# Normalising the attention probabilities: two scaled identities on GpSimd, or one row multiply each on GpSimd and VectorE

## The reference, cut to what matters

```python
p = jnp.exp(s - m)
denom = jnp.sum(p, axis=-1, keepdims=True) + jnp.exp(sink - m)
o = jnp.einsum('bnkgqs,bnskd->bnqkgd', (p / denom).astype(v.dtype), vb)
```

```python
p_w = masked_softmax(jnp.einsum('bgrqd,bgkd->bgrqk', qb, kw), m_w)
o_w = jnp.einsum('bgrqk,bgkd->bgrqd', p_w.astype(vw.dtype), vw)
return gb[:, 0][..., None] * o_c + gb[:, 1][..., None] * o_s + gb[:, 2][..., None] * o_w
```

## Time and profile before

| what | value |
| --- | --- |
| median of 3 runs | 4002.84 us (4000.92 to 4006.6) |
| profiled execution: span from first to last instruction | 4004.4 us |
| its own time outside the span | not listed; the span stands for it |
| PE busy, share | 3909.7 us, 98% |
| DVE | 2736.3 us, 68% |
| ACT | 1987.8 us, 50% |
| POOL | 212.2 us, 5% |
| mean granted TensorE clock | 0.991 |

### The profile page before, as it was taken

How to read it: one execution, slowest core, us unless ns; L and a number is a source line. 1 busy time by engine, 2 the same in 40 slices (tenths; PEclk the granted TensorE clock), 3 DMA queues, 4 the chain that set the end, 5 groups by cost and what they waited for, 6 DMA issues and landing times.

```text
span 4004.4 us, 78708 instructions
## 1 busy us (share of the span) xinstructions
PE 3909.7 (98%) x34150; PEld 3793.3 (95%) x34150; DVE 2736.3 (68%) x4071; ACT 1987.8 (50%) x2620; POOL 212.2 (5%) x277
## 2 busy tenths in 40 slices
PE   8999999999999999999999999999999999999999
PEld 8979999889998999999997999999998899999999
DVE  6566665666655656567555799956756699974855
ACT  5445444454544545465435545754444544764443
POOL 0011000110002000010023000000000000000000
PEclk9999999999999999999998999999999999999999
DMA  6534555345555455534550455456654455455754
GB/s 237 192 115 151 192 190 190 133 148 195 181 194 182 160 199 184 195 133 173 191 204 34 159 194 181 177 199 233 229 196 153 158 177 193 175 182 202 265 199 158
DMA packets 114791, 720.78 MB, mean 180 GB/s; under 512 B 13328, under 2 KB 13664, under 8 KB 32784
## 3 DMA queue, kind: packets, MB, share of 16 engines
q1 hardware_dynamic: 90144, 652.25, 45.9%
q10 hardware_dynamic: 19200, 37.01, 2.5%
q0 software_dynamic: 5104, 26.49, 1.9%
HBM read 692.48 MB, written 23.22 MB: 179 GB/s over the span
## 4 chain that ended last, share of the span: by engine, by line
PE 87%; DVE 7%; ACT 4%; issue 1%; POOL 0%; DMA 0%; ACTq 0%; DVEq 0%; POOLq 0%
PE psum L655 26%; PE psum L657 26%; PE psum L656 26%; PE psum L1408 3%; DVE slab_low L1916 2%; ACT slab_high L1427 2%; DVE h_parts L2219 1%; PE psum L1065 1%; PE psum L1048 1%; PE psum L875 1%; PE psum L1078 1%; ACT room L1670 1%; DVE room L2248 0%; DVE room L2253 0%; PE psum L1349 0%
## 5 line engine op out<-in xcount | busy, mean ns | idle before, releaser
L1916 DVE TENSOR_TENSOR slab_low<-slab,slab_high 128x2048 fp32r<-128x2048 f32 x622 | 1423.2, 2289 | 738.8 <-ACT slab_high L1427 736.6
L655 PE MATMUL psum<-h_parts,slab_high 128*128 128x256 f32 x5632 | 1578.2, 280 | 28.9 <-DVE h_parts L2219 18.6
L1427 ACT ACTIVATE slab_high<-slab 128x2048 fp32r<-128x2048 f32 x622 | 1189.3, 1912 | 785.4 <-PE psum L657 721.1
L656 PE MATMUL psum<-h_parts,slab_high 128*128 128x256 f32 x5632 | 1556.5, 276 | 0.0
L657 PE MATMUL psum<-h_parts,slab_low 128*128 128x256 f32 x5632 | 1556.1, 276 | 0.0
L655 PEld LDWEIGHTS psum<-h_parts,slab_high 128*128 128x128 f32 x5632 | 1063.5, 189 | 48.8 <-issue 24.0
L655 PE MATMUL psum<-hidden_parts,slab_high 128*128 128x256 f32 x3840 | 1063.5, 277 | 11.4 <-DVE hidden_parts L2166 4.8
L656 PEld LDWEIGHTS psum<-h_parts,slab_high 128*128 128x128 f32 x5632 | 1063.5, 189 | 2.4 <-issue 2.2
L657 PEld LDWEIGHTS psum<-h_parts,slab_low 128*128 128x128 f32 x5632 | 1062.8, 189 | 0.0
L656 PE MATMUL psum<-hidden_parts,slab_high 128*128 128x256 f32 x3840 | 1058.0, 276 | 0.0
L657 PE MATMUL psum<-hidden_parts,slab_low 128*128 128x256 f32 x3840 | 1058.0, 276 | 0.0
(11 more groups left out here) (346 smaller groups left out, 3326.0 us busy)
## 6 DMA issues: line engine op xcount, KB each, us to landing
slab<-in_up SPq DMA_DIRECT2D x176, 1024.0 KB, 4.8
slab<-in_keys_up SPq DMA_DIRECT2D x128, 1024.0 KB, 4.8
slab<-in_keys_down SPq DMA_DIRECT2D x128, 1024.0 KB, 4.8
slab<-in_down SPq DMA_DIRECT2D x88, 1024.0 KB, 4.8
slab<-in_w_in SPq DMA_DIRECT2D x16, 1024.0 KB, 4.8
slab<-in_wq SPq DMA_DIRECT2D x16, 1024.0 KB, 4.8
peer_gates<-room ACTq DMA_DIRECT2D x64, 256.0 KB, 2.3
room<-peer_gates ACTq DMA_DIRECT2D x64, 256.0 KB, 5.4
```

The lines of the kernel that those rows point to most:

```text
L655: nc.tensor.matmul(out, lhs[0], rhs[0], start=first, stop=False, **options)
L656: nc.tensor.matmul(out, lhs[0], rhs[1], start=False, stop=False, **options)
L1427: nc.scalar.activation(k.high[m % PARTS][:, 0:width], k.slabs[m % RING][:, 0:width], ACT.Copy).then_inc(k.rounded.up())
L1916: nc.vector.tensor_tensor(k.low[m % RING][:, 0:width], k.slabs[m % RING][:, 0:width], k.high[m % PARTS][:, 0:width], ALU.subtract).then_in ...
```

## The change

In the first mixers and the sparse stage, the diagonals go. DVE still forms the quotients (reciprocal, and gate product in the sparse stage), now signals them (`quotients`), waits for its own signal, and multiplies the second head's row of probabilities in place. GpSimd waits for the same signal and multiplies the first head's row in place. PE waits for both and turns the rows with `transpose`, as the forgetting stage does. The wait for a stale quotient buffer stays, on the new signal. The buffers of the diagonals go, at the end of their stage's memory, so that nothing else moves. The forgetting stage keeps its instructions; only its DVE step's signal has another name.

```diff
 PE, attend:
-            if "diagonal" in v.items[n]:
-                nc.tensor.wait_ge(k.diagonal_pool.sem, k.diagonal_pool.at(n + 1))
-            else:
-                nc.tensor.wait_ge(k.normed.sem, k.normed.at(n + 1))
+            nc.tensor.wait_ge(k.normed.sem, k.normed.at(n + 1))
+            if "shared" in v.items[n]:
+                nc.tensor.wait_ge(k.normed_pool.sem, k.normed_pool.at(n + 1))
...
-                    if "diagonal" in v.items[n]:
-
-                        mm = nc.tensor.matmul(k.banks[6][:, at:at + P], v.probs[:, n % 5, e, kt * P:(kt + 1) * P], v.diagonals[:, n % 3, e, :],
-                                              start=True, stop=True)
-                        continue
                     mm = nc.tensor.transpose(k.banks[6][:, at:at + P], v.probs[:, n % 5, e, kt * P:(kt + 1) * P], k.const("ident"))
 DVE, normalise:
-            if "diagonal" in it and n >= 6:
-                nc.vector.wait_ge(k.diagonal_pool.sem, k.diagonal_pool.at(n - 5))
-            if "diagonal" in it and "gate" not in it:
-                nc.vector.reciprocal(small[:, 8:10], small[:, 4:6]).then_inc(k.normed.up())
-                continue
-            self.then(nc.vector.reciprocal(small[:, 8:10], small[:, 4:6]))
-            if "diagonal" in it:
-                nc.vector.tensor_tensor(small[:, 8:10], small[:, 8:10], it["gate"], ALU.mult).then_inc(k.normed.up())
-                continue
-            for e in range(2):
+            if "shared" in it and n >= 6:
+                nc.vector.wait_ge(k.normed_pool.sem, k.normed_pool.at(n - 5))
+            quotient = nc.vector.reciprocal(small[:, 8:10], small[:, 4:6])
+            if "gate" in it:
+                self.then(quotient)
+                quotient = nc.vector.tensor_tensor(small[:, 8:10], small[:, 8:10], it["gate"], ALU.mult)
+            quotient.then_inc(k.quotients.up())
+            nc.vector.wait_ge(k.quotients.sem, k.quotients.at(n + 1))
+            for e in (1,) if "shared" in it else (0, 1):
                 row = v.probs[:, n % 5, e, 0:keys]
                 mul = nc.vector.tensor_scalar(row, row, small[:, 8 + e:9 + e], None, ALU.mult)
             mul.then_inc(k.normed.up())
 POOL:
-    def diagonals(self, v, n):
-        k, nc = self.k, self.k.nc
-        nc.gpsimd.wait_ge(k.normed.sem, k.normed.at(n + 1))
-        if n >= 3:
-            nc.gpsimd.wait_ge(k.turned.sem, k.turned.at(n - 2))
-        for e in range(2):
-            made = nc.gpsimd.tensor_scalar(v.diagonals[:, n % 3, e, :], k.const("ident"), v.stats[:, n % 6, 8 + e:9 + e], None, ALU.mult)
-        made.then_inc(k.diagonal_pool.up())
+    def normalise_first(self, v, n):
+        k, nc = self.k, self.k.nc
+        row = v.probs[:, n % 5, 0, 0:P * (v.items[n]["tile"] + 1)]
+        nc.gpsimd.wait_ge(k.quotients.sem, k.quotients.at(n + 1))
+        nc.gpsimd.tensor_scalar(row, row, v.stats[:, n % 6, 8:9], None, ALU.mult).then_inc(k.normed_pool.up())
```

More of the change, by code:

```diff
@@ L255, in __init__ @@
         self.centred, self.conv_activated = signal("centred"), signal("conv_activated")
-        self.diagonal_pool = signal("diagonal_pool")
+        self.quotients, self.normed_pool = signal("quotients"), signal("normed_pool")
         self.kept, self.absd, self.logs, self.masked = signal("kept"), signal("absd"), signal("logs"), signal("masked")
@@ L383, in mixer_one_views @@
     attention_views(k, v)
-    v.diagonals = k.carve(3, 2, P)
     assert k.taken <= k.room_words - DC * 2 * T
@@ L390, in mixer_one_views @@
             n = P * (i + 1)
-            it = dict(diagonal=True, tile=i, pair=pair, q=v.q[:, pair, :], bias=v.bias[:, 2 * pair:2 * pair + 2, P - i * P:T], scale=v.scales[:, i:i + 1])
+            it = dict(shared=True, tile=i, pair=pair, q=v.q[:, pair, :], bias=v.bias[:, 2 * pair:2 * pair + 2, P - i * P:T], scale=v.scales[:, i:i + 1])
             if pair < 4:
@@ L570, in nsa_views @@
                     bias=k.const("causal")[:, P - i * P:T].unsqueeze(1).to_broadcast([P, 2, P * (i + 1)]), scale=v.scales[:, i:i + 1],
-                    first=branch == 0, last=branch == 1, whole=TT * pair + i, diagonal=True))
+                    first=branch == 0, last=branch == 1, whole=TT * pair + i, shared=True))
     v.starts = [NSA_FIRST + n for n in range(32)]
@@ L2660, in mixer_one @@
         for n in range(len(v.items)):
-            self.diagonals(v, n)
-    def diagonals(self, v, n):
+            self.normalise_first(v, n)
+    def normalise_first(self, v, n):
         k, nc = self.k, self.k.nc
-        nc.gpsimd.wait_ge(k.normed.sem, k.normed.at(n + 1))
-        if n >= 3:
-            nc.gpsimd.wait_ge(k.turned.sem, k.turned.at(n - 2))
-        for e in range(2):
-            made = nc.gpsimd.tensor_scalar(v.diagonals[:, n % 3, e, :], k.const("ident"), v.stats[:, n % 6, 8 + e:9 + e], None, ALU.mult)
-        made.then_inc(k.diagonal_pool.up())
+        row = v.probs[:, n % 5, 0, 0:P * (v.items[n]["tile"] + 1)]
+        nc.gpsimd.wait_ge(k.quotients.sem, k.quotients.at(n + 1))
+        nc.gpsimd.tensor_scalar(row, row, v.stats[:, n % 6, 8:9], None, ALU.mult).then_inc(k.normed_pool.up())
     def conv(self, v):
```

## The result

The changed kernel takes 4014.07 us (median of 12 runs), the kernel before 4003.64 in the same comparison: a ratio of 1.0023, with a 95% interval of 1.0014 to 1.0031 (the two medians alone give 1.0026). So it is 10.4 us slower. One of its twelve runs took 7830.48 us, and one run each of experiments 3 and 7 took 14012.92 and 8860.03; the medians count these runs, the ratios do not. The spans of the two profiles differ by 8.1 us, 2.3 less than the medians, and it is these 8.1 that the traces can place.

What follows compares the result with a forecast made beforehand. It took a loop of DVE and ACT to bound the first mixers, with PE and the loop nearly level in the later sparse stage. First mixers +3.6, sparse stage +3.3 and clock +4.1 made +11.0 on 4002.84: 4014 us, range 3999 to 4035.

Steps and rivals of the forecast that it cites:

- The multiply's price: In the loop of DVE and ACT, DVE's added multiply costs 0.32 us per tile 0 item, 0.405 per tile 1.
- First mixers, +3.6 forecast: Four runs of eight items in the first mixers each lose 0.89 us net, together +3.6 us.
- The loop's term: In a first-mixer run, seven items delay a successor, 2.50 us, less 0.40 hidden in a slab remainder's wait.
- the end gives back 1.21: At a run's end the last three turns have no DVE work ahead; shorter transposes save 1.21 us there.
- Sparse stage without the clock, +3.3 forecast: Sparse stage: first twelve items 0, later 20 items +4.5 us, end gives back 1.21, leaving +3.3.
- The first twelve items, put at 0: Sparse stage's first twelve items: 4.35 us more on DVE, taken up by 4.23 us of waits for PE's scores.
- 20 items were put at 4.5: Sparse stage's later 20 items: +1.81 us for every eight, 4.5 us in all.
- 1.09 us of waits in eight items: Later sparse items: three adds in eight wait for PE's scores, 1.09 us that would offset DVE's added 2.90.
- The clock, +4.1 forecast: Sparse stage: an idler PE brings two falls to half clock of 6.8 us, 2.1 us each, +4.1 us.
- 1.37 us more an item: Later sparse items at half clock: PE needs 4.54 us an item against the loop's 3.17, 1.37 more.
- The wait for GpSimd: Rival: DVE's multiply is held off by GpSimd's at the same moment, 0.59 us an item, +35 us, 4049; chance 0.07.
- The rule weighed in the prediction: On PE: transposes don't count as busy time like matmuls and don't engage full clock, so PE would look idler than 0.78.

Runs made afterwards that it cites:

- experiment 3: The changed kernel, but PE turns the rows with a matmul by the identity in place of a transpose: 4022.33 us, ratio 1.0038 to the kernel before.
- experiment 7: The changed kernel, but DVE's row multiply comes one tick later in the sparse stage alone: 4003.46 us, ratio 0.9996 to the kernel before.
- experiment 2: The changed kernel, but DVE multiplies both heads' rows and GpSimd none: 4024.55 us, ratio 1.0047 to the kernel before.
- experiment 4: The late version: the changed kernel, but DVE multiplies an item's second row one tick later, behind the next add and maximum: 3995.52 us, ratio 0.998 to the kernel before.
- experiment 6: The changed kernel, but DVE's row multiply comes one tick later in the two first mixers alone: 4005.93 us, ratio 0.9999 to the kernel before.
- experiment 1: The changed kernel, but GpSimd multiplies both heads' rows and DVE none: 3997.89 us, ratio 0.9981 to the kernel before.
- experiment 10: The changed kernel, but DVE multiplies a tick later in the first mixers and GpSimd multiplies both rows in the sparse stage: 3997.76 us, ratio 0.9982 to the kernel before.
- experiment 8: The kernel before the change, unchanged, run once more for a second profile: 4012.32 us.

## Why the prediction was right, and which terms were off

The forecast was 4014, between 3999 and 4035, with slower by over 0.2% as the likelier side; measured were 4014.07 and +0.23%. The direction and the mechanism hold: experiments 2, 4, 6 and 7 show the price of the multiply in the loop. That the sum hit to the microsecond is partly luck, since terms missed in opposite senses (the first mixers came to more, the sparse stage with its clock to 2.7 in place of 7.4) and the two profiles lie 2.3 us closer than the medians. By the readings below, the terms in the pair of profiles were +3.9 for the first mixers without the clock (3.6 forecast), +1.1 for the sparse stage without it (3.3) and +2.8 for the clock (4.1). The medians may hold more of the clock than this pair does, as the clocks under experiment 4 show.

- **The multiply's price** (0.32 and 0.405 an item) held, as 0.32 and 0.39. In the sparse stage free steps from add to add grew from 2.16 to 2.48 us at tile 0 and from 2.90 to 3.29 at tile 1.
- **First mixers, +3.6 forecast, +5.1 measured.** The loop's term held: the first runs grew by 1.90 and 2.05 us (forecast 2.10), the second by 1.66 and 1.58, since there two steps with a slab's remainder, and not one, took the multiply in (4.46 to 4.42 us and 4.30 to 4.28 in the first mixer). What failed is the step "the end gives back 1.21". Between the two runs only 0.27 came back, both times; without half clock there (experiments 1, 2 and 6) it was 0.44. Behind the second run 1.17 came back in the first mixer and 0.34 in the second, where PE stood at half clock behind the last item (831.5 to 834.9).
- **Sparse stage without the clock, +3.3 forecast.** The first twelve items, put at 0, became 0.6 us shorter: some of their steps had been stretched by waits for PE at half clock. The 19 steps behind them grew by 2.66, where 20 items were put at 4.5. The step that failed is the reading of 1.09 us of waits in eight items. A bracketed wait counts from the end of the instruction ahead, while a free add starts before that end, and a step with a slab's remainder hid waiting too. By steps it was 2.90 - 1.15 = 1.75 us in eight: tile 1 steps of 3.27 and 3.53 fell to 3.29, where a free one had been 2.90.
- **The clock, +4.1 forecast.** Half clock came as forecast, 17.0, 6.8, 3.4 and 3.4 us of it in the stretches below, but the step "1.37 us more an item" failed: PE's item at half clock was put at its mean work with the output projection, and the longest stretch lies in the ticks that have none. There PE worked 13.9 of 17 us, and no add waited for it. In the second stretch, in a tick with the output projection, one step was 4.42 us where later ones like it took 4.24.

```profile
2125.20:2142.20 17.00, 13.90 (x69) 7.50 (x66) 10.24 (x30) 7.70 (x30) 5.27 (x6) 0.50 0.01 1
2145.70:2152.50 6.80, 6.68 (x32) 4.86 (x32) 4.78 (x12) 5.35 (x15) 1.65 (x2) 0.50 0.00 1
2196.90:2200.30 3.40, 3.40 (x15) 2.40 (x15) 2.35 (x7) 2.26 (x5) 1.34 (x2) 0.51 0.00 0
2220.80:2224.20 3.40, 3.40 (x16) 3.28 (x16) 1.78 (x1) 2.24 (x3) 0.00 (x0) 0.51 0.02 5
```

It cost most where PE ends last. From the last add to the slab took 61.08 us before, 61.66 after, and 60.04 to 60.08 in experiments 1, 2, 4 and 7, which have no half clock behind the last add: the last stretch above cost 1.6 us, more than the 1.0 that the end gives back without it. Among the items it is not always free: experiment 6 has the change's sparse stage with its half clock elsewhere, and there adds did wait for scores, two of them at the ends of steps of 4.78 and 5.02 us in place of 4.24, just behind half clock:

```profile
2148.05 0.75 DVE L2241 SCALAR_TENSOR_TENSOR room<-psum,room,consts 128x512 f32<-128x512 f32 x1 [0.44 <-PE psum L1070]
...
2198.21 0.75 DVE L2241 SCALAR_TENSOR_TENSOR room<-psum,room,consts 128x512 f32<-128x512 f32 x1 [0.69 <-PE psum L1070]
```

Half clock did come to the first mixers, where the prediction had put none, four times:

```profile
282.00:285.40 3.40, 3.40 (x15) 2.48 (x14) 3.30 (x7) 0.97 (x6) 0.95 (x1) 0.50 0.02 5
316.10:319.50 3.40, 3.40 (x17) 2.03 (x15) 1.94 (x7) 1.95 (x9) 1.08 (x1) 0.50 0.00 0
787.10:790.60 3.50, 3.50 (x20) 3.22 (x20) 3.33 (x9) 0.23 (x1) 0.95 (x1) 0.51 0.00 0
831.50:834.90 3.40, 3.40 (x20) 3.11 (x20) 2.71 (x6) 0.55 (x3) 0.95 (x1) 0.50 0.02 5
```

By the lengths above, the first and the third, at the end of a first run, cost 0.17 us each (0.27 came back in place of 0.44). The second lies inside a run of items, which took 23.80 us with it and 23.72 without it in the other mixer. The fourth, behind the last item, cost 1.17 - 0.34 = 0.83. That is some 1.2 us over both mixers.

- **The wait for GpSimd** did not come about. DVE's multiply started 0.20 us after the quotient, as forecast, and took 0.29 us at 128 columns and 0.35 or 0.36 at 256 in all 32 sparse items; GpSimd's own grew longer beside it. Groups by line of POOL in the sparse stage, the change and then the late version:

```profile
L2659 POOL TENSOR_SCALAR room<-room 128x256 f32<-128x256 f32 x16 | 17.6, 1100 | 40.9 <-DVE room L2266 40.9
L2659 POOL TENSOR_SCALAR room<-room 128x128 f32<-128x128 f32 x16 | 12.7, 792 | 53.2 <-DVE room L2266 53.2
```

```profile
L2673 POOL TENSOR_SCALAR room<-room 128x256 f32<-128x256 f32 x16 | 15.2, 951 | 39.8 <-DVE room L2267 39.8
L2673 POOL TENSOR_SCALAR room<-room 128x128 f32<-128x128 f32 x16 | 10.3, 644 | 51.3 <-DVE room L2267 51.3
```

On average that is 0.15 us more where DVE's multiply starts just ahead of it (by 0.05 or 0.06 us). Taken singly, GpSimd's went from 0.60 to 0.70 us at 128 columns and from 0.92 to 1.08 at 256, and from 0.71 to 0.95 where DVE's `hidden_parts` step follows. This agrees in its direction with the Trainium skill (SBUF — State Buffer, Who interferes with whom): who issues second is held up, and that is GpSimd here, on whom nobody waits in this stage. That it is held for the whole of DVE's instruction the rows do not show: 0.10 and 0.16 us are less than the 0.23 and 0.30 by which DVE's multiply outlasts GpSimd's start.

## What to carry to other kernels

Ask of an added instruction where it stands in the loop that sets the pace, rather than how busy its engine is: 0.32 to 0.39 us an item, on an engine with a quarter of its time free in these stages, made 18.5 us of difference over 64 items here between two places in the order, one in the loop and one in a wait a tick later. Measure what a wait is worth by the step from one turn of the loop to the next, with a free step beside it, and not by the bracket alone. And price half clock by place: where PE has time to spare it cost nothing (17 us in a row), in ticks with a projection 0.2 to 0.8 us, and behind the last item, where PE ends last, 0.8 to 1.6 us for 3.4. Last, look at the clock of every run before a difference of a few us is put down to one cause.

## What the runs showed of the chip

- **Twice the transposes, no half clock.** The rule weighed in the prediction (the Trainium skill, TensorE: Matmul & The Clock Gate, Part 4: PE-mode transpose) has transposes not count as busy time in the way a matmul does. Here the late version has two stretches at half clock in the first mixers (3.5 us each, from 279.9 and 771.4), and so have experiments 6 and 10, whose first mixers are the same; with each transpose doubled there is none, and with identity matmuls of about the same length none. The traces do not bear the rule out, but this is weak: each kernel has one profile, and the kernel before, with its matmuls, had no half clock in these stages in one profile and a stretch of 6.9 us in the other.
- **In the changed loop, identity matmuls did not save it.** Experiment 3 has PE's work of before and still three stretches at half clock in the mixers (3.4 us each, from 283.9, 792.5 and 836.9), all around the last item of a run. PE's longer waits for DVE may be the reason; no run tests that apart.
- **Half clock can repeat closely.** The change and experiment 7, whose first mixers are the same, have their four stretches there at the same times to 0.1 us, though they are two kernels and two executions. The two executions of the kernel before (experiment 8) did not repeat.
